# Transforming back the Hyena convolution by time parity, with frequencies f and 255-f folded on the vector engine

## The chip, the cores and the metric

One core of one Trainium2 chip. The metric is the device time of one execution in microseconds (us), the median of several runs. A core has five engines with queues of their own: TensorE (PE, with its weight loads shown apart as PEld), VectorE (DVE), ScalarE (ACT), GpSimd (POOL) and SyncE (SP), which here issues the loads of weights.

## The reference

Two layers of an encoder over 256 tokens of width 2048. Each layer runs three mixers on the same stream (an S5 state-space scan, an order-2 Hyena long convolution, latent attention), gates and lifts their outputs, and ends in a LayerNorm. The change lies in the Hyena mixer alone:

```python
def hyena_mixer(u3, conv_w, conv_b, filt_f, bias):
    uc = short_conv3(u3, conv_w, conv_b)
    v, x1, x2 = jnp.split(uc, 3, axis=-1)
    z = v
    for n, gate in enumerate((x1, x2)):
        z_f = jnp.fft.rfft(z, n=2 * L, axis=1)
        conv = jnp.fft.irfft(z_f * filt_f[:, n], n=2 * L, axis=1)[:, :L]
        z = gate * (conv + bias[n] * z)
    return z
```

Here L is 256 and there are 1024 channels. The kernel does not call an FFT: it multiplies by tables of cosines and sines at the 256 odd half frequencies (f + 0.5) / 512, which gives the same linear convolution.

## The kernel before

**Weights and the planner of the stages.** All weights come as 184 blocks per layer of 128 x 2048 numbers. SyncE loads each block as two halves into a ring of four half-slots. ScalarE rounds each quarter (128 x 512) of a block to a high part WH (`make_wh`, L370), VectorE subtracts it from the block to get the low part WL (`make_wl`, L384), and only when a half's low part stands may TensorE use that half; TensorE then makes three products for each tile (high by high, high by low, low by high; L1481). WH and WL are single buffers of four quarters. So ScalarE can write a quarter of the next block only when TensorE has used that quarter of this block (`parts_used`), and VectorE follows ScalarE. The order of the work on every engine is written out by hand; nothing is scheduled at run time.

**The Hyena stage.** Its work is spread over 24 steps `k`, each with one block of the lift (48 matmuls) behind it: 12 steps for each of the two convolutions, `o = k // 12`, `s_ = k % 12`. The stages of one convolution by step are: filter taps (0, 3), their transform (2, 5), the transposes of z (6), the forward transform of z (7 to 9), and the inverse transform (10, 11). The 256 frequencies lie as two halves `m` of 128 partitions, the 1024 channels as two halves of 512 columns. On TensorE a step is: the Hyena matmuls of the step, then the block of the step. On VectorE a step is: the low parts of quarters 0 and 1 of the next block, the Hyena work of the step, the low parts of quarters 2 and 3, and then more Hyena work (short convolutions) and every third step `mix_in`.

**What the change touches.** `product(o, m, half)` (L949 to L969) multiplies the transform of z, which lies in two PSUM banks, by the filter's transform: four products of 128 x 512 (L961 to L964), a sum (L966) and a difference (L968), into YRE and YIM. It is called four times for each convolution: for m = 0 in step 7, for m = 1 and channel half 0 in step 8, for m = 1 and half 1 in step 9. `inverse(o, n)` on TensorE (L1785 to L1798) is called in steps 10 and 11 for four of the eight tiles of channels each. It waits until all eight results of the convolution's products stand, and makes four float32 matmuls for each tile, with 128 channels as stationary operand and a table of 256 time steps as moving one (L1793). A float32 matmul shows as two records in the trace. `unconv(o, m)` on VectorE reads each finished tile from its bank in steps 10 and 11: bias (L978), scale and add (L980), gate (L984, or L987 and L988). The next user of the banks waits for L980. `put` at the end of the kernel fills the tables in the constants CON, which GpSimd's queue loads at the start (L414).

Matmuls that only release a semaphore do it through `pending`: the release rides on the next matmul that is issued. The last quarter of a block is so given back by the first matmul of what follows the block.

Of the kernel before, what the change touches and what calls it, by code (L numbers as in the profile page):

```python
# [30 lines left out]
ALU = mybir.AluOpType  # L31
# [3 lines left out]
P = 128  # L35
# [76 lines left out]
    "out":  [2, 2, 2, 2, 2, 2, 2, 2],  # L112
}
ZIN = 24 + WT
DVE_STEPS, DVE_S5_STEPS = 457, 23
ACT_STEPS, ACT_S5_STEPS = 8, 1
PER_LAYER = [sum(FILLS[s][b] for s in STAGES) for b in range(8)]

# [13 lines left out]
def columns(*parts):  # L132
    at, out = 0, {}
    for name, n in parts:
        out[name] = (at, at + n)
        at += n
    return out, at
# [3 lines left out]
                   ("conv_w0", 24), ("conv_w1", 24), ("conv_w2", 24), ("conv_b", 24), ("hy_bias", 16),  # L141
                   ("q_norm", 4), ("kv_norm", 4), ("ln_g", DT), ("ln_b", DT),
                   ("b1", 1), ("b2", 1), ("freq0", 1), ("freq1", 1))
CP, CP_N = columns(("cos", 2 * T), ("sin", 2 * T), ("icos", 2 * T), ("isin", 2 * T), ("token4", HOPS),
                   ("ident", P), ("ones", P), ("inv_freq", 1),
                   ("half_pi", 1))

# [30 lines left out]
def trunk(nc, x, blocks, lp, bc, w1, w2, b3, decay, feats, pT, pos, consts, out):  # L178
    with ExitStack() as ctx:
# [35 lines left out]
        def con(name):  # L215
            return CON[:, CP[name][0]:CP[name][1]]
# [7 lines left out]
        xh, xl = split(XH, DT), split(XL, DT)  # L224
        xx = XX[:].rearrange("p (r k t) -> p r k t", r=2, k=DT)
        dft_cos, dft_sin = con("cos").rearrange("p (k f) -> p k f", k=2), con("sin").rearrange("p (k f) -> p k f", k=2)
        idft_cos, idft_sin = con("icos").rearrange("p (k f) -> p k f", k=2), con("isin").rearrange("p (k f) -> p k f", k=2)
        ident, ones, half_pi, token4 = con("ident"), con("ones"), con("half_pi"), con("token4")


# [258 lines left out]
        def _(dve):  # L489
# [14 lines left out]
            with dve.Fori(0, DEPTH) as layer:  # L504
# [445 lines left out]
                def product(o, m, half):  # L950

                    b = 4 + 2 * half
                    n = hyc(o, "fwd", m, b)
                    n2 = hyc(o, "fwd", m, b + 1)
                    zc, zs = bank[b][:, :], bank[b + 1][:, :]
                    oc = slice(half * CW, (half + 1) * CW)
                    fr, fi = frt[:, m, oc], fit[:, m, oc]
                    t1, t3 = TM[:, 0:CW], TM[:, CW:2 * CW]
                    full(b, "hyc", n)
                    full(b + 1, "hyc", n2)  # L960
                    st.did(v.tensor_tensor(yret[:, m, oc], zc, fr, ALU.mult))  # L961
                    free(v.tensor_tensor(yimt[:, m, oc], zc, fi, ALU.mult), b)
                    st.did(v.tensor_tensor(t1, zs, fi, ALU.mult))
                    free(v.tensor_tensor(t3, zs, fr, ALU.mult), b + 1)  # L964
                    st.wait()
                    v.tensor_tensor(yret[:, m, oc], yret[:, m, oc], t1, ALU.add).then_inc(yf_ready, 1)  # L966
                    out_of(b + 1, "hyc", n2)
                    v.tensor_tensor(yimt[:, m, oc], yimt[:, m, oc], t3, ALU.subtract).then_inc(yf_ready, 1)  # L968
                    dve.wait_ge(yf_ready, layer * 16 + (o * 8 + m * 4 + half * 2 + 2))  # L969

                def unconv(o, m):

                    b, n = 4 + m % 4, hyc(o, "inv", m // 4, 4 + m % 4)
                    z, gate, t = bct[:, m, :], bct[:, 8 * (o + 1) + m, :], TM[:, 0:T]
                    if o and m:

                        dve.wait_ge(yb_ready, layer * 8 + m)
                    st.did(v.tensor_scalar(t, z, par("hy_bias", o * 8 + m), None, ALU.mult)); st.wait()  # L978
                    full(b, "hyc", n)
                    free(v.scalar_tensor_tensor(out=t, in0=bank[b][:, 0:T], scalar=NS[:, o * 8 + m:o * 8 + m + 1], in1=t,  # L980
                                                op0=ALU.mult, op1=ALU.add), b)
                    out_of(b, "hyc", n)
                    if o == 0:
                        v.tensor_tensor(z, t, gate, ALU.mult).then_inc(z_in, 1)  # L984
                        dve.wait_ge(z_in, layer * ZIN + (16 + m + 1))
                    else:
                        st.did(v.tensor_tensor(t, t, gate, ALU.mult)); st.wait()  # L987
                        v.tensor_tensor(z, t, PROJt[:, 42 + m, :], ALU.mult).then_inc(yb_ready, 1)  # L988
# [11 lines left out]
                for k in range(24):  # L1000
                    o, s_ = k // 12, k % 12
                    make_wl(dve, v, layer, B_LIFT + 24 + k + 1, halves=(0,))

                    if s_ in (0, 3):
                        taps_out(o, s_ // 3)
                    if s_ == 1 and o == 0:

                        dve.wait_ge(yh_ready, layer * 4 + 2)
                        v.tensor_tensor(YCL, YC, YCH.bitcast(F32), ALU.subtract).then_inc(yl_ready, 1)
                    if s_ in (7, 8, 9):  # L1010
                        if s_ == 8:
                            full(6, "hyc", hyc(o, "sums", 0, 6))
                            free(v.reciprocal(NS[:, o * 8:o * 8 + 8], bank[6][:, 0:8]), 6)
                        product(o, (0, 1, 1)[s_ - 7], (0, 0, 1)[s_ - 7])
                    if s_ in (10, 11):
                        for m in range((s_ - 10) * 4, (s_ - 10) * 4 + 4):
                            unconv(o, m)
                    if o == 0:
                        for m in {1: (0,), 2: (1, 2), 4: (4, 5), 5: (6, 7), 6: (9, 10)}.get(s_, ()):
                            short_conv(m)  # L1020
                    else:
                        for m in {1: (17, 18), 2: (19, 20), 4: (21, 22), 5: (23,)}.get(s_, ()):
                            short_conv(m)
                    make_wl(dve, v, layer, B_LIFT + 24 + k + 1, halves=(1,))

                    if s_ in (0, 3):
                        even_odd(o, s_ // 3)
                    if s_ in (1, 4):
                        sums(o, s_ // 3)
                    if s_ == 7:  # L1030
                        product(o, 0, 1)
                    if o == 0:
                        for m in {2: (3,), 5: (8,), 6: (11,), 8: (12,), 9: (13, 14, 15), 11: (16,)}.get(s_, ()):
                            short_conv(m)
                    if k % 3 == 2:
                        mix_in(k // 3, "hyc", k // 3)
# [384 lines left out]
        def _(pe):  # L1421
# [6 lines left out]
            with pe.Fori(0, DEPTH) as layer:  # L1428
# [355 lines left out]
                        done(ins, b)  # L1784

                def inverse(o, n):
                    pe.wait_ge(yf_ready, layer * 16 + (o * 8 + 8))
                    for c in range(4 * n, 4 * n + 4):
                        b = 4 + c % 4
                        take_bank(b, "hyc", hyc(o, "inv", n, b))  # L1790
                        for k in range(4):
                            r, m = k // 2, k % 2
                            ins = mm(bank[b][:, 0:T], yft[r][:, m, c * P:(c + 1) * P], (idft_sin if r else idft_cos)[:, m, :],  # L1793
                                     start=(k == 0), stop=(k == 3))
                            if k < 3:
                                release(ins)
                        done(ins, b)
# [173 lines left out]
def shape_constants():  # L1971

    con = np.zeros((P, CP_N), np.float32)

    def put(name, a):
        con[:, CP[name][0]:CP[name][1]] = a
    t, f = np.arange(T)[:, None], np.arange(T)[None, :]
    ang = 2 * np.pi * (f + 0.5) * t / (2 * T)
    fold = lambda a: a.reshape(2, P, T).transpose(1, 0, 2).reshape(P, 2 * T)
    put("cos", fold(np.cos(ang)))  # L1980
    put("sin", fold(np.sin(ang)))
    put("icos", fold(np.cos(ang.T) / T))
    put("isin", fold(-np.sin(ang.T) / T))
    put("token4", STEP * np.arange(HOPS))
    put("ident", np.eye(P))
    put("ones", 1.0)
    half = 32
    inv = np.float32(10000.0) ** (-np.arange(half, dtype=np.float32) / np.float32(half))
    put("inv_freq", np.tile(inv, 4)[:, None])
    put("half_pi", HALF_PI)  # L1990

    n_ch = 2 * W
    tl = np.linspace(0.0, 1.0, T, dtype=np.float32)[:, None]
    w = np.float32(2.0 * math.pi) * np.arange(T, dtype=np.float32)[:, None] / np.float32(T)
    bands = np.linspace(1e-4, 15, 16, dtype=np.float32)[None, :]
    feats = np.concatenate([tl, np.cos(bands * w), -np.sin(bands * w)], axis=-1).astype(np.float32)
    deltas = np.linspace(math.log(0.01) / 1.5, math.log(0.01) / 0.3, n_ch, dtype=np.float32)
    decay = np.exp(-tl * np.abs(deltas)).astype(np.float32)
    decay = decay.reshape(2, P, CHUNKS, CW).transpose(2, 1, 0, 3).reshape(CHUNKS, P, 2 * CW)
    return con, np.ascontiguousarray(feats.T), np.ascontiguousarray(decay)  # L2000
# [61 lines left out]
```

## Time and profile before

| | us |
|---|---|
| median of 3 runs (2844.43 to 2846.63) | 2844.88 |
| the profiled execution, its own time | 2844.58 |
| its span, first to last instruction | 2842.3 |
| TensorE busy | 2696.7 (95%) |
| VectorE busy | 1860.9 (65%) |
| ScalarE busy | 1310.6 (46%) |
| mean granted TensorE clock | 0.979 of full |

Lines of the page are read as: source line, engine, operation, output from inputs, count, busy time, mean duration of one in ns, and the idle time just before with what ended it. "WL L384" as a releaser is a low part of a weight block.

### The profile page before, as it was taken

Reading aid. Unit: us, or ns where it says so; the run is one execution under the profiler, and the core shown is the slowest. Engines: PE = TensorE matmul, PEld = TensorE weight load, DVE = VectorE, ACT = ScalarE, POOL = GpSimd, SP = SyncE. Lnnn points to the kernel's source line nnn. Section 1 sums busy time; section 2 is a strip of 40 time slices with the busy share of each in tenths; the row PEclk is TensorE's granted clock in tenths of the full one; section 3 lists DMA queues with packets and bytes.
Section 4 is the critical chain, followed back from the end, with each engine's and each line's share of the span. In section 5 each row is a group of like instructions: output and inputs, shape, how many; then the busy total and the mean of one; then the engine's idle time right before and its main releaser. Section 6 shows DMA issues by size and latency. Waiting matters only on the chain.

```text
span 2842.3 us, 49160 instructions
## 1 busy us (share of the span) xinstructions
PE 2696.7 (95%) x17320; PEld 2385.5 (84%) x17320; DVE 1860.9 (65%) x3290; ACT 1310.6 (46%) x2353; POOL 109.5 (4%) x202
## 2 busy tenths in 40 slices
PE   5899999989999999999979999999899999999998
PEld 4798999877997778998768899998789877799986
DVE  5878878734557766556577877876345677665655
ACT  3455555534554233453444555556245432334535
POOL 1100000000000000000021000000000000000000
PEclk9999999999999999999989999999999999999999
DMA  6444444423443333555554444443344523245554
GB/s 210 155 150 148 146 149 144 146 106 135 149 158 118 104 100 120 184 177 172 163 171 146 147 150 145 150 142 120 135 133 143 170 97 112 98 134 180 178 173 146
DMA packets 115388, 412.30 MB, mean 145 GB/s; under 512 B 15332, under 2 KB 15354, under 8 KB 114736
## 3 DMA queue, kind: packets, MB, share of 16 engines
q1 hardware_dynamic: 106992, 391.17, 41.2%
q0 software_dynamic: 8256, 19.26, 2.1%
q8 instruction: 89, 1.46, 0.2%
q14 instruction: 51, 0.42, 0.1%
HBM read 404.07 MB, written 6.29 MB: 144 GB/s over the span
## 4 chain that ended last, share of the span: by engine, by line
PE 87%; DVE 6%; issue 3%; ACT 3%; DMA 1%; DVEq 0%; POOLq 0%; POOL 0%; ACTq 0%; SPq 0%
PE bank L1481 30%; PE bank L1509 18%; PE bank L1511 9%; PE bank L1858 6%; PE bank L1463 5%; PE bank L1793 2%; PE bank L1602 2%; PE bank L1579 2%; PE bank L1561 2%; PE bank L1757 2%; PE bank L1780 1%; PE bank L1546 1%; PE bank L1596 1%; PE bank L1670 1%; DVE WL L384 1%
## 5 line engine op out<-in xcount | busy, mean ns | idle before, releaser
L370 ACT ACTIVATE WH<-ring 128x512 fp32r<-128x512 f32 x1364 | 858.2, 631 | 1277.1 <-PE bank L1481 599.4
L384 DVE TENSOR_TENSOR WL<-ring,WH 128x512 fp32r<-128x512 f32 x852 | 577.5, 690 | 528.9 <-ACT WH L370 526.3
L1509 PE MATMUL bank<-XX,WH 128*128 128x512 f32 x2304 | 825.5, 401 | 61.1 <-DVE XX L502 23.3
L1481 PE MATMUL bank<-XX,WH 128*128 128x256 f32 x3712 | 682.8, 286 | 13.0 <-DVE WL L384 8.5
L1511 PE MATMUL bank<-XX,WL 128*128 128x256 f32 x2304 | 646.0, 280 | 0.0
L1481 PEld LDWEIGHTS bank<-XX,WH 128*128 128x128 f32 x3712 | 580.5, 192 | 31.2 <-issue 24.3
L1509 PEld LDWEIGHTS bank<-XX,WH 128*128 128x128 f32 x2304 | 437.5, 190 | 163.8 <-issue 36.2
L1481 PE MATMUL bank<-XX,WL 128*128 128x256 f32 x1856 | 526.2, 284 | 0.0
L375 DVE TENSOR_TENSOR WL<-ring,WH 128x512 fp32r<-128x512 f32 x512 | 350.9, 688 | 139.9 <-ACT WH L370 135.9
L1511 PEld LDWEIGHTS bank<-XX,WL 128*128 128x128 f32 x2304 | 439.5, 191 | 0.0
L1481 PEld LDWEIGHTS bank<-XX,WL 128*128 128x128 f32 x1856 | 357.0, 192 | 0.0
L1463 PE MATMUL bank<-ARENA,ring 128*128 128x256 f32 x704 | 158.8, 388 | 19.4 <-ACT ARENA L1288 17.5
L1463 PEld LDWEIGHTS bank<-ARENA,ring 128*128 128x128 f32 x704 | 135.0, 195 | 42.6 <-issue 21.8
L1858 PE MATMUL bank<-WL,MIXH 128*128 128x512 f32 x256 | 101.7, 397 | 0.0
L1858 PE MATMUL bank<-WH,MIXL 128*128 128x512 f32 x256 | 101.2, 395 | 0.0
L1858 PE MATMUL bank<-WH,MIXH 128*128 128x512 f32 x256 | 101.2, 395 | 0.0
L1481 PE MATMUL bank<-YCH,WH 128*128 128x256 f32 x256 | 79.0, 309 | 0.0
L1481 PE MATMUL bank<-YAH,WH 128*128 128x256 f32 x256 | 75.0, 293 | 0.0
L1481 PE MATMUL bank<-YCL,WH 128*128 128x256 f32 x256 | 74.6, 291 | 0.0
L1481 PE MATMUL bank<-YCH,WL 128*128 128x256 f32 x256 | 74.5, 291 | 0.0
L1481 PE MATMUL bank<-YAH,WL 128*128 128x256 f32 x256 | 71.9, 281 | 0.0
L1481 PE MATMUL bank<-YAL,WH 128*128 128x256 f32 x256 | 71.9, 281 | 0.0
(299 smaller groups left out, 3561.2 us busy)
## 6 DMA issues: line engine op xcount, KB each, us to landing
ring<-in_blocks SPq DMA_DIRECT2D x738, 512.0 KB, 3.3
ARENA<-in_bc POOLq DMA_DIRECT2D x2, 2048.0 KB, 8.1
ARENA<-in_decay POOLq DMA_DIRECT2D x8, 512.0 KB, 4.6
ARENA<-in_x SPq DMA_DIRECT2D x1, 2048.0 KB, 9.4
u_scratch<-ARENA POOLq DMA_DIRECT2D x16, 128.0 KB, 2.5
ARENA<-u_scratch POOLq DMA_DIRECT2D x64, 32.0 KB, 2.9
y_scratch<-ARENA POOLq DMA_DIRECT2D x16, 128.0 KB, 2.0
ARENA<-y_scratch POOLq DMA_DIRECT2D x64, 32.0 KB, 2.7
```

Source lines behind the costliest of these rows:

```text
L370: nc.scalar.activation(wh[q], raw(which[0], q), ACT.Copy).then_inc(wh_ready[q], 1)
L375: nc.vector.tensor_tensor(wl[q], raw(which[0], q), wh[q].bitcast(F32), ALU.subtract).then_inc(w_used[slot(which[0], q // 2)], 1)
L384: vec.tensor_tensor(wl[q], raw(which[0], q), wh[q].bitcast(F32), ALU.subtract).then_inc(w_used[slot(which[0], half)], 1)
L1463: ins = mm(o, w[:, (w0 + i) * P:(w0 + i + 1) * P], rhs(i), start=i == 0, stop=i == k - 1)
L1481: ins = mm(o, w_, x_, start=start and i == 0 and n == 0, stop=stop and i == 7 and n == 2)
L1509: ins = mm(bank[b][:, :], h, xx[:, :, k, :], start=(k == 0), stop=(k == DT - 1), skip_group_check=True)
L1511: ins = mm(bank[b][:, 0:T], l, xh[:, k, :], start=False, stop=(k == DT - 1), skip_group_check=True)
L1561: ins = mm(o, ET[:, q % 2 * CW + i * P:q % 2 * CW + (i + 1) * P], u4(q), start=True, stop=True)
L1579: ins = mm(bank[4 + d][:, q * P:(q + 1) * P], b, f, start=(r == 0), stop=(r == 1))
L1602: ins = mm(o, f, x_, start=False, stop=(d == 1 and r == 1))
L1757: ins = mm(bank[4 + q][:, :], tab, ED[:, (im * 2 + t) * CW:(im * 2 + t + 1) * CW], start=(t == 0), stop=(t == 1))
L1858: ins = mm(bank[b][:, :], x_[:, k, tok[t]], w_[q], start=False, stop=(k == 15 and n == 2), skip_group_check=True)
```

## The change

The table columns of frequency are reordered, so that partition p of the first half holds frequency p and partition p of the second half holds frequency 255 - p. After the product of the second half, `fold` replaces the two halves of YRE by their sum and by the first minus the second, and the same for YIM: two additions and two scaled additions of 128 x 512 for each half of the channels. The inverse then makes even time steps from the one and odd time steps from the other: for each tile of channels four float32 matmuls as before, but with 128 moving columns each, the even steps to the first 128 columns of the bank and the odd steps to the second. `unconv` reads them in the interleaved order again. The inverse of a half of the channels now waits for that half's fold alone, and the inverse tables are half as large.

```diff
-CP, CP_N = columns(("cos", 2 * T), ("sin", 2 * T), ("icos", 2 * T), ("isin", 2 * T), ("token4", HOPS),
+CP, CP_N = columns(("cos", 2 * T), ("sin", 2 * T), ("icos", T), ("isin", T), ("token4", HOPS),
...
                     st.wait()
-                    v.tensor_tensor(yret[:, m, oc], yret[:, m, oc], t1, ALU.add).then_inc(yf_ready, 1)
+                    st.did(v.tensor_tensor(yret[:, m, oc], yret[:, m, oc], t1, ALU.add))
                     out_of(b + 1, "hyc", n2)
-                    v.tensor_tensor(yimt[:, m, oc], yimt[:, m, oc], t3, ALU.subtract).then_inc(yf_ready, 1)
-                    dve.wait_ge(yf_ready, layer * 16 + (o * 8 + m * 4 + half * 2 + 2))
+                    st.did(v.tensor_tensor(yimt[:, m, oc], yimt[:, m, oc], t3, ALU.subtract))
+                    st.wait()
+
+                def fold(o, half):
+
+                    oc = slice(half * CW, (half + 1) * CW)
+                    for y in (yret, yimt):
+                        st.did(v.tensor_tensor(y[:, 0, oc], y[:, 0, oc], y[:, 1, oc], ALU.add))
+                    for back, y in ((1, yret), (0, yimt)):
+                        st.wait(back)
+                        v.scalar_tensor_tensor(out=y[:, 1, oc], in0=y[:, 1, oc], scalar=-2.0, in1=y[:, 0, oc],
+                                               op0=ALU.mult, op1=ALU.add).then_inc(yf_ready, 1)
...
-                    free(v.scalar_tensor_tensor(out=t, in0=bank[b][:, 0:T], scalar=NS[:, o * 8 + m:o * 8 + m + 1], in1=t,
-                                                op0=ALU.mult, op1=ALU.add), b)
+                    by_parity = t.rearrange("p (s r) -> p s r", r=2)
+                    free(v.scalar_tensor_tensor(out=by_parity, in0=bank[b][:, 0:T].rearrange("p (r s) -> p s r", r=2),
+                                                scalar=NS[:, o * 8 + m:o * 8 + m + 1], in1=by_parity, op0=ALU.mult, op1=ALU.add), b)
...
                         product(o, (0, 1, 1)[s_ - 7], (0, 0, 1)[s_ - 7])
+                        if s_ > 7:
+                            fold(o, s_ - 8)
...
-                    pe.wait_ge(yf_ready, layer * 16 + (o * 8 + 8))
+                    pe.wait_ge(yf_ready, layer * 8 + (o * 4 + 2 * n + 2))
...
                         for k in range(4):
-                            r, m = k // 2, k % 2
-                            ins = mm(bank[b][:, 0:T], yft[r][:, m, c * P:(c + 1) * P], (idft_sin if r else idft_cos)[:, m, :],
-                                     start=(k == 0), stop=(k == 3))
+                            odd, r = k // 2, k % 2
+                            cols = slice(odd * P, (odd + 1) * P)
+                            ins = mm(bank[b][:, cols], yft[r][:, odd ^ r, c * P:(c + 1) * P], (idft_sin if r else idft_cos)[:, cols],
+                                     start=(r == 0), stop=(r == 1))
...
+    order = np.concatenate([np.arange(P), 255 - np.arange(P)])
+    by_parity = np.concatenate([np.arange(0, T, 2), np.arange(1, T, 2)])
+    put("cos", fold(np.cos(ang)[:, order]))
+    put("sin", fold(np.sin(ang)[:, order]))
+    put("icos", np.cos(ang.T)[:P, by_parity] / T)
+    put("isin", -np.sin(ang.T)[:P, by_parity] / T)
```

The number of counted VectorE steps in a layer (`DVE_STEPS`) goes from 457 to 481 with it.

## Rows read from the trace of the kernel before

**Rows 1.** The page: busy time of each engine, share of the span, instructions.

```profile
PE 2696.7 (95%) x17320; PEld 2385.5 (84%) x17320; DVE 1860.9 (65%) x3290; ACT 1310.6 (46%) x2353; POOL 109.5 (4%) x202
```

**Rows 2.** The page: shares by engine of the chain that ended last.

```profile
PE 87%; DVE 6%; issue 3%; ACT 3%; DMA 1%; DVEq 0%; POOLq 0%; POOL 0%; ACTq 0%; SPq 0%
```

**Rows 3.** Instruction groups by line and shape, whole span: busy us, mean ns, idle.

```profile
L384 DVE TENSOR_TENSOR WL<-ring,WH 128x512 fp32r<-128x512 f32 x852 | 577.5, 690 | 528.9 <-ACT WH L370 526.3 <-DVE ARENA L547 0.7 <-DVE ARENA L900 0.6
...
L1793 PE MATMUL bank<-CON,ARENA 128*128 128x256 f32 x256 | 58.9, 389 | 9.5 <-DVE ARENA L968 9.5
...
L769 DVE TENSOR_TENSOR_SCAN ARENA<-ARENA 128x256 f32<-128x256 f32 x64 | 40.5, 675 | 0.0
...
L729 DVE SCALAR_TENSOR_TENSOR ARENA<-ARENA 64x640 f32<-64x640 f32 x32 | 26.1, 816 | 0.5
...
L980 DVE SCALAR_TENSOR_TENSOR ARENA<-bank,NS,ARENA 128x256 f32<-128x256 f32 x32 | 15.5, 484 | 1.5
...
L968 DVE TENSOR_TENSOR ARENA<-ARENA 128x512 f32<-128x512 f32 x16 | 10.9, 684 | 0.0
```

**Rows 4.** PE timeline, layer 0, o = 1: start, length, work, [idle before, releaser].

```profile
1064.97 3.60 PE L1780 MATMUL bank<-ARENA,CON 128*128 128x512 f32 x8
...
1076.67 7.17 PE L1793 MATMUL bank<-CON,ARENA 128*128 128x256 f32 x32 [2.36 <-DVE ARENA L968]
...
1089.43 7.20 PE L1793 MATMUL bank<-CON,ARENA 128*128 128x256 f32 x32
...
1108.80 0.58 PE L1481 MATMUL bank<-XX,WH 128*128 128x256 f32 x2 [2.77 <-DVE WL L384]
```

**Rows 5.** Windows: length, then PE, PEld, DVE, ACT, POOL busy, clock, DMA.

```profile
933.81:976.21 42.40, 39.69 (x239) 33.56 (x239) 31.95 (x66) 9.34 (x16) 0.00 (x0) 1.00 0.26 88
1063.83:1108.06 44.23, 39.20 (x251) 34.73 (x250) 30.02 (x62) 9.37 (x16) 0.00 (x0) 1.00 0.26 84
2340.64:2383.02 42.38, 39.69 (x239) 33.57 (x239) 31.95 (x65) 9.35 (x16) 0.00 (x0) 1.00 0.27 88
2470.66:2516.60 45.94, 40.83 (x251) 35.85 (x249) 30.08 (x62) 9.35 (x16) 0.00 (x0) 0.96 0.24 81
```

**Rows 6.** DVE timeline, layer 0, o = 0: its waits in that stretch.

```profile
948.04 0.69 DVE L384 TENSOR_TENSOR WL<-ring,WH 128x512 fp32r<-128x512 f32 x1 [0.80 <-ACT WH L370]
...
955.94 0.69 DVE L384 TENSOR_TENSOR WL<-ring,WH 128x512 fp32r<-128x512 f32 x1 [2.87 <-ACT WH L370]
957.50 0.69 DVE L384 TENSOR_TENSOR WL<-ring,WH 128x512 fp32r<-128x512 f32 x1 [0.87 <-ACT WH L370]
...
968.60 0.69 DVE L384 TENSOR_TENSOR WL<-ring,WH 128x512 fp32r<-128x512 f32 x1 [3.64 <-ACT WH L370]
970.14 0.69 DVE L384 TENSOR_TENSOR WL<-ring,WH 128x512 fp32r<-128x512 f32 x1 [0.85 <-ACT WH L370]
```

**Rows 7.** Timeline of DVE: two of the products in a row.

```profile
1064.39 0.68 DVE L962 TENSOR_TENSOR ARENA<-bank,ARENA 128x512 f32<-128x512 f32 x1
1064.98 0.68 DVE L963 TENSOR_TENSOR ARENA<-bank,ARENA 128x512 f32<-128x512 f32 x1
```

**Rows 8.** Timeline of PE in the S5 stage: float32 matmuls of 128 columns.

```profile
126.43 1.95 PE L1579 MATMUL bank<-ARENA 128*128 128x128 f32 x16
128.13 0.48 PE L1509 MATMUL bank<-XX,WH 128*128 128x512 f32 x1
```

**Rows 9.** Timeline of PE, layer 1, o = 1: the first inverse.

```profile
2483.46 8.86 PE L1793 MATMUL bank<-CON,ARENA 128*128 128x256 f32 x32 [2.36 <-DVE ARENA L968]
```

**Rows 10.** Windows: granted clock (PEclk) behind two waits of PE.

```profile
1107.00:1112.00 5.00, 3.20 (x16) 3.20 (x17) 4.86 (x10) 3.35 (x4) 0.55 (x1) 0.71 0.37 125
2483.00:2489.00 6.00, 5.54 (x18) 4.60 (x19) 1.71 (x3) 0.90 (x2) 0.00 (x0) 0.72 0.25 87
```

**Rows 11.** DMA issues at the start: KB, us from issue to landing.

```profile
ARENA<-in_x SPq DMA_DIRECT2D x1, 2048.0 KB, 9.4
...
CON<-in_consts POOLq DMA_DIRECT2D x1, 1185.0 KB, 10.8
```

More of the change, by code:

```diff
@@ L114 @@
 ZIN = 24 + WT
-DVE_STEPS, DVE_S5_STEPS = 457, 23
+DVE_STEPS, DVE_S5_STEPS = 481, 23
 ACT_STEPS, ACT_S5_STEPS = 8, 1
@@ L226, in trunk @@
         dft_cos, dft_sin = con("cos").rearrange("p (k f) -> p k f", k=2), con("sin").rearrange("p (k f) -> p k f", k=2)
-        idft_cos, idft_sin = con("icos").rearrange("p (k f) -> p k f", k=2), con("isin").rearrange("p (k f) -> p k f", k=2)
+        idft_cos, idft_sin = con("icos"), con("isin")
         ident, ones, half_pi, token4 = con("ident"), con("ones"), con("half_pi"), con("token4")
@@ L1979, in shape_constants @@
     fold = lambda a: a.reshape(2, P, T).transpose(1, 0, 2).reshape(P, 2 * T)
[L1980 to L1983, printed above, removed]
+    order = np.concatenate([np.arange(P), 255 - np.arange(P)])
[4 more added lines that the diff above has]
+    put("isin", -np.sin(ang.T)[:P, by_parity] / T)
     put("token4", STEP * np.arange(HOPS))
```

## Prediction

> **What bounds the kernel now.** I read the page first: TensorE is busy 95% of the span, VectorE 65% [rows 1], and the chain that ended last is 87% TensorE and 6% VectorE [rows 2]. So over the whole span a us taken from TensorE is worth nearly a us. That is an average, and the change sits in four short places: two layers, two convolutions each, steps 8 to 12. There the reader is to look at two things. In the timeline of TensorE, the first inverse of a convolution waits 2.36 us for the last subtraction of `product` (L968), and soon after the second inverse TensorE waits 2.77 us for a low weight part, WL, from VectorE [rows 4]. And in the windows from the product of step 8 to the end of the last `unconv`, VectorE is busy 31.95 of 42.4 us in the first convolution (o = 0) and 30.0 of 44.2 or 45.9 us in the second (o = 1), well above its share of 65% [rows 5]. So these stretches have two lines of work of nearly one length. TensorE takes 39.7 us in the one and VectorE 32.0 us plus the waits for WH that TensorE's pace gives it [rows 5, 6]. A cut on TensorE alone is given back only until VectorE's idle time in the stretch is used up.
>
> **TensorE: half the columns.** The inverse is 128 instructions in 256 records, 58.9 us busy [rows 3], in eight calls of 32 records; an undisturbed one shows 7.17 us with a tail of 0.4 [rows 4], so 6.8 us. The count stays, with 128 columns instead of 256. The S5 stage has float32 matmuls of just that shape, 128 x 128 by 128 columns, each with its own weights: 16 records start at 126.43 and the next work starts at 128.13, 0.106 us a record [rows 8]. So a call takes 32 x 0.106 = 3.4 us and saves 3.4 us. That the weight loads don't become the bound is shown by the same row, which has one load for each record too.
>
> **TensorE: the wait before the first inverse.** It needed the products of step 9; now it needs only the fold of step 8, which ends about 2.4 us later than the product of step 8 does now, more than 3 us before TensorE is through with the block of step 9. The 2.36 us go. The wait also held back the release of the block's last quarter, which rides on the first matmul of the inverse. The second inverse needs the fold of step 9, which ends while TensorE is in the block of step 10. If nothing else were late, one convolution would gain 2.36 + 2 x 3.4 = 9.2 us.
>
> **VectorE: the folds.** Each fold is two additions and two scaled additions of 128 x 512. A step from one product to the next is 0.60 us [rows 7], and a scaled addition costs what an addition does: 640 columns in 816 ns against 512 in 684 to 690 is 1 ns a column [rows 3]. The waits in it are for the instruction before the last, or one whose result is due when its turn comes, at 0.1 us or less. The drain behind the last subtraction was there before. So 2.4 us a fold, 4.8 us a convolution, 19.2 us in all. The stretch from the product of step 8 onward takes both folds.
>
> **What the two together give.** With both folds in, I follow VectorE through one stretch (o = 0, layer 0), each instruction at its present length. Fold 0 moves everything behind it by 2.4 us, so the last low part of the block of step 9 stands at about 941.2, just before TensorE needs it. Fold 1 puts the low parts of quarters 2 and 3 for the block of step 10 about a us behind TensorE's need. From there every wait for WH of VectorE is gone: it comes to each after ScalarE has been there. The four waits of `unconv`'s time vanish, and TensorE instead waits for VectorE, about 1 us in the block of step 10 and 2.7 us in that of step 11. So the stretch gets shorter by VectorE's waits less the folds. The waits of o = 0 are five: 0.80 + 2.87 + 0.87 + 3.64 + 0.85 = 9.03 us [rows 6]. The window has 42.40 - 31.95 = 10.45 us idle [rows 5]; the other 1.4 us are the small gaps between dependent instructions, which stay. The same difference in the other windows gives 14.21 - 1.4 = 12.8 (layer 0, o = 1), 10.43 - 1.4 = 9.0 (layer 1, o = 0) and 15.86 - 1.4 = 14.5 (layer 1, o = 1). Less 4.8 each: 4.2 + 8.0 + 4.2 + 9.7 = 26.1 us. This is below TensorE's 9.2 in each (in the last TensorE also gets back a slow piece of clock, below), so VectorE is the bound. Behind the stretches both engines stand as far from each other as now: the taps of o = 1 follow the last `unconv` of o = 0 as before, and the 2.77 us wait after o = 1 stays, or grows to about 3.3 us.
>
> **The read by parity.** L980 reads its bank with a hop of 128 numbers after each and takes 484 ns now, 32 times [rows 3]. No row has such a read. Below, nothing is lost: the count of elements is the same (a gain is excluded, since no element is saved). Above, the nearest rows are those of an instruction that takes two cycles or so an element: the scan, 675 ns for 256 columns [rows 3], against the 425 ns that 684 ns for 512 come to with 1 ns a column: 0.25 us more. The read's own row stands at the lower end, the only slow row at the upper, and neither is nearer in kind, so I take the middle, 0.125 us. VectorE is the bound there, so all count: 32 x 0.125 = 4.0 us, bounds 0 and 8.0.
>
> The Trainium skill (Vector Engine (DVE) Microarchitecture Reference, section 5.2, "The SBUF access granule: adjacent pairs") speaks against the edit: a port streams at full rate only while its elements come in adjacent pairs, and one source that hops every element cost 1.73 instead of 1.054 ns a column. It says so of SBUF; here the source is PSUM, which no row shows. By it each read would cost 0.17 us more (an estimate from that page), 5.5 us in all instead of 4.0, and the time would be 2825.6.
>
> **The clock.** After the wait of 2.36 us in layer 1, o = 1 the inverse shows 8.86 us instead of 7.17 [rows 9], and the granted clock is 0.72 over that window: part of it at the lower level, 1.2 GHz. The wait of 2.77 us is followed by the same (0.71) [rows 10]. The first is already in the 9.7 above. New waits of up to 2.7 us in the block of step 11 of o = 0, in both layers, may bring one each: 2 x 1.7 us. As VectorE is the bound there, I count half: 1.7 us lost, bounds 0 and 3.4.
>
> **The constants.** CON shrinks by 512 of 2370 columns, 256 of 1185 KB. The whole load took 10.8 us [rows 11] in a time when the queues share the bandwidth; at 0.4 MB/us for all of them, as 2 MB of x, the first weights and this arrive in some 12 us, 0.25 MB are 0.6 us at most. The first work waits for it; I take 0.4 us, bounds 0 and 0.6.
>
> The semaphores and the host's reordering of tables cost nothing. The forward transform has the same instructions with other table columns.
>
> **The sum.** 26.1 + 0.4 - 4.0 - 1.7 = 20.8 us less. The profiled execution took 2844.58 us, with 2842.3 us of span, 0.3 us under the median of 2844.88; I count from the median: 2824.1 us. Its own range, from the bounds of the terms: 2844.9 - 26.7 = 2818 to 2844.9 - (26.1 - 8.0 - 3.4) = 2830.
>
> **The rivals.**
> - *TensorE keeps its whole cut.* If VectorE's work can move off the path (the folds hide in its waits and the low parts still come in time), 4 x 9.2 + 1.7 + 0.4 = 38.9 us, 2806. For it: TensorE is 95% busy. Against it: the waits of VectorE (9.0) are less than 4.8 + 9.2. 6%.
> - *Half width doesn't halve the time.* If a record of the inverse is held by something like the weight load's own length, 0.19 us instead of 0.106, a call takes 6.1 us and a convolution gains 2.36 + 2 x 0.7 = 3.8 us: 15.2 + 1.7 + 0.4 = 17.3, less about 2 of the parity read that the slack doesn't hide, 2830. Against it: [rows 8]. The edit then does not do what it says. 7%.
> - *The clock.* Each of the waits that now fall on TensorE (two to each convolution) starts a piece at the lower level, at 1.7 us, all on the path: six more than counted, 10 us, so 2834. For it: both rows of [rows 10]. Against it: the waits of 2.36 us of [rows 4] cost nothing. 16%.
> - *Slower: the loop of WH and WL.* ScalarE's high part waits for TensorE, VectorE's low part for ScalarE, TensorE for VectorE. If the added work on VectorE delays each turn of that loop and the waits for WH stay as they are, they are not idle time to be used, and folds and parity reads are added whole: 19.2 + 4.0 = 23 us, 2868. It decides when less than 5.8 us of a stretch's 9.0 to 14.5 us of waits can be used. For it: VectorE's waits all name ScalarE [rows 6]. Against it: ScalarE is busy only 9.3 us in each stretch [rows 5], and its own wait is for TensorE, which comes sooner. 5%.
>
> **How the numbers follow.** The forecast has 66%. Range 2814 to 2834: the forecast with its bounds, the clock's case to its value, and part of the first rival's way; outside are the loop, most of the first rival and the far half of the clock. A run of this kernel can tell 0.2%, 5.7 us, from no change. Below 2839 lie the forecast, the first two rivals and nearly all of the clock's case: faster 91%. Within 0.2%: 5%, the far end of the clock's case and a mild form of the loop. Slower: 4%.
>
> **What would show it.** L1793 at 256 records and about 31 us busy instead of 58.9 (half width right; 48 would be the second rival). No wait before the first inverse. VectorE idle in the four windows down to the small gaps of 1.4 us, with the waits on L370 gone and waits of TensorE on "WL L384" in their place in the blocks of steps 10 and 11: the bound has changed hands. The fold's four instructions at 0.69 us each, 32 in all of 22 us busy. L980 at 0.6 us if the middle is right, 0.48 or 0.73 at the ends. If VectorE still has several us of waits in the windows and TensorE has none, the first rival is right; if both have waits, the loop is.

## The result and the profile after

The changed kernel takes 2827.94 us (median of 4 runs, 2823.75 to 2829.64) against 2845.29 us before (4 runs): ratio 0.9936, 95% interval 0.9919 to 0.9954. That is 17.4 us or 0.6% faster. Two later groups of five runs gave 2827.27 and 2824.77 us, ratios 0.9940 (0.9926 to 0.9953) and 0.9925 (0.9911 to 0.9938). The profiled execution is the shortest of the first four: 2823.75 us, 20.8 us less than the profiled execution before. Its span is 2822.2 us, 20.1 us less. So its trace shows some 3 us more of gain than the medians.

The page, busy time of each engine (compare [rows 1]), and the chain that ended last (compare [rows 2]):

```profile
PE 2676.2 (95%) x17320; PEld 2370.0 (84%) x17320; DVE 1878.4 (67%) x3322; ACT 1310.4 (46%) x2353; POOL 109.5 (4%) x202
...
PE 85%; DVE 8%; issue 3%; ACT 3%; DMA 1%; DVEq 0%; POOLq 0%; POOL 0%; ACTq 0%; SPq 0%
```

TensorE lost 20.5 us of busy time, VectorE gained 17.5, and the chain moved by 2% from the one to the other. The groups of instructions that changed (compare [rows 3]; the inverse is now L1807, the read by parity L991, the folds L975 and L978):

```profile
L1807 PE MATMUL bank<-CON,ARENA 128*128 128x128 f32 x256 | 37.1, 304 | 12.4 <-DVE ARENA L991 11.3 <-DVE ARENA L962 1.0
...
L991 DVE SCALAR_TENSOR_TENSOR ARENA<-bank,NS,ARENA 128x256 f32<-128x256 f32 x32 | 15.5, 483 | 1.5
...
L975 DVE TENSOR_TENSOR ARENA<-ARENA 128x512 f32<-128x512 f32 x16 | 10.3, 688 | 0.3
L978 DVE SCALAR_TENSOR_TENSOR ARENA<-ARENA 128x512 f32<-128x512 f32 x16 | 10.3, 685 | 0.0
```

The first line has the surprise: the 9.5 us of waits for L968 before the inverse are gone, and 12.4 us of waits are there instead, 11.3 of them for L991, which is `unconv`, and 1.0 for L962, which is `product`. The timeline of TensorE places them (first convolution of layer 0, then the second; compare [rows 4]):

```profile
943.15 1.95 PE L1807 MATMUL bank<-CON,ARENA 128*128 128x128 f32 x16
945.60 2.35 PE L1807 MATMUL bank<-CON,ARENA 128*128 128x128 f32 x16 [0.50 <-DVE ARENA L962]
...
958.05 6.70 PE L1807 MATMUL bank<-CON,ARENA 128*128 128x128 f32 x32 [3.80 <-DVE ARENA L991]
```

```profile
1072.35 3.73 PE L1807 MATMUL bank<-CON,ARENA 128*128 128x128 f32 x32
...
1083.43 1.16 PE L1807 MATMUL bank<-CON,ARENA 128*128 128x128 f32 x8 [0.41 <-DVE ARENA L991]
1085.34 1.16 PE L1807 MATMUL bank<-CON,ARENA 128*128 128x128 f32 x8 [0.76 <-DVE ARENA L991]
1087.17 1.16 PE L1807 MATMUL bank<-CON,ARENA 128*128 128x128 f32 x8 [0.67 <-DVE ARENA L991]
...
1100.50 0.70 PE L1494 MATMUL bank<-XX,WH 128*128 128x256 f32 x2 [2.81 <-DVE WL L384]
```

An undisturbed call is 3.73 us, 0.24 of it tail, where it was 7.17: the columns were halved and so was the time. But both calls of a convolution write banks 4 to 7. The first call of the first convolution stops for 0.50 us in its middle, for a bank that the product of step 9 (L962) has not read out yet. And the second call may write a bank only when `unconv` has read the first call's tile from it. In the first convolution `unconv` stands on VectorE behind three short convolutions (4.4 us), and TensorE waits 3.80 us for it. The call behind this wait takes 6.70 us instead of 3.73, because of the clock. Windows of the two such places, layer 0 and layer 1 (length, then PE, PEld, DVE, ACT and POOL busy, granted clock, DMA share, GB/s; compare [rows 10]):

```profile
958.00:962.00 4.00, 3.95 (x18) 3.95 (x19) 3.60 (x9) 0.90 (x2) 0.00 (x0) 0.50 0.36 131
2357.00:2361.00 4.00, 3.91 (x22) 3.91 (x23) 3.60 (x10) 0.90 (x2) 0.00 (x0) 0.61 0.39 131
```

0.50 is the lower of the clock's two levels, 1.2 GHz, for the whole window. Finally the four stretches from the product of step 8 to the end of the last `unconv` (compare [rows 5]):

```profile
932.85:974.49 41.64, 36.63 (x240) 31.56 (x240) 36.49 (x74) 9.35 (x16) 0.00 (x0) 0.92 0.25 89
1062.08:1099.78 37.70, 33.12 (x251) 30.03 (x249) 34.39 (x70) 9.34 (x16) 0.00 (x0) 1.00 0.30 98
2331.87:2372.20 40.33, 35.32 (x240) 30.24 (x239) 36.49 (x74) 9.34 (x16) 0.00 (x0) 0.96 0.28 92
2458.29:2496.01 37.72, 33.17 (x251) 30.08 (x250) 34.41 (x70) 9.35 (x16) 0.00 (x0) 1.00 0.31 98
```

They are 157.4 us together, 174.95 before: 17.6 us less, of the 20.1 us by which the span shrank. The gain is very uneven: 0.8 and 2.1 us in the first convolutions, 6.5 and 8.2 us in the second. VectorE is busy 4.3 to 4.5 us more in each. Its idle time is 5.15, 3.31, 3.84 and 3.31 us; with 1.3 to 1.4 of small gaps in each, 3.7, 2.0, 2.4 and 2.0 us are still waits. The forecast had none left. They stand behind the bank wait, and they are waits for WH, as before. The longest in the first stretch:

```profile
966.86 0.69 DVE L384 TENSOR_TENSOR WL<-ring,WH 128x512 fp32r<-128x512 f32 x1 [2.90 <-ACT WH L370]
```

### The profile page after: what moved, and what is told of

It is laid out like the page before. It is cut to its first block, busy times and chain, and to the rows that moved or that the text cites. A ratio compares the mean times of both kernels' runs of the same rounds, so it can differ in the third digit from the quotient of the medians.

```text
span 2822.2 us, 49206 instructions
## 1 busy us (share of the span) xinstructions
PE 2676.2 (95%) x17320; PEld 2370.0 (84%) x17320; DVE 1878.4 (67%) x3322; ACT 1310.4 (46%) x2353; POOL 109.5 (4%) x202
## 4 chain that ended last, share of the span: by engine, by line
PE 85%; DVE 8%; issue 3%; ACT 3%; DMA 1%; DVEq 0%; POOLq 0%; POOL 0%; ACTq 0%; SPq 0%
PE bank L1494 29%; PE bank L1522 18%; PE bank L1524 9%; PE bank L1872 6%; PE bank L1476 5%; PE bank L1615 2%; PE bank L1592 2%; PE bank L1574 2%; PE bank L1770 2%; DVE WL L384 1%; PE bank L1793 1%; PE bank L1559 1%; PE bank L1609 1%; PE bank L1683 1%; PE bank L1708 1%
## 5 line engine op out<-in xcount | busy, mean ns | idle before, releaser
L1476 PE MATMUL bank<-ARENA,ring 128*128 128x256 f32 x704 | 158.8, 387 | 18.7 <-ACT ARENA L1301 17.4
```

What stands on the lines that cost most here:

```text
L1476: ins = mm(o, w[:, (w0 + i) * P:(w0 + i + 1) * P], rhs(i), start=i == 0, stop=i == k - 1)
```

## The experiments

Three groups, each on one chip with runs of the kernel before beside them. "Under before" is the difference of the medians of a group.

| run | median us | under before | ratio, 95% interval |
|---|---|---|---|
| a1_after_again | 2827.27 | 17.4 | 0.9940, 0.9926 to 0.9953 |
| a2_split_wait | 2834.08 | 10.6 | 0.9962, 0.9949 to 0.9976 |
| a3_no_fold | 2814.40 | 30.3 | 0.9895, 0.9879 to 0.9910 |
| a4_wide | 2840.93 | 3.7 | 0.9985, 0.9976 to 0.9994 |
| b1_after_third | 2824.77 | 20.7 | 0.9925, 0.9911 to 0.9938 |
| b2_late | 2827.00 | 18.5 | 0.9931, 0.9918 to 0.9945 |
| b3_banks | 2816.52 | 29.0 | 0.9896, 0.9881 to 0.9912 |
| b4_banks_late | 2818.67 | 26.8 | 0.9904, 0.9888 to 0.9919 |
| c1_banks_again | 2814.41 | 31.6 | 0.9890, 0.9874 to 0.9905 |
| c2_banks_no_fold | 2807.43 | 38.5 | 0.9868, 0.9853 to 0.9883 |
| c3_banks_pool | 2823.44 | 22.5 | 0.9921, 0.9907 to 0.9934 |
| c4_sbuf_hop | 2824.05 | 21.9 | 0.9923, 0.9908 to 0.9938 |

**The changed kernel again.**

> The changed kernel once more, as the reference point of this group. Its runs so far spread from 2823.8 to 2829.6 us. Both theories: 17 to 21 us under the kernel before. If the spread is that of pieces at the lower TensorE clock, the profile with more such pieces is the longer one, 1.7 us for each 3.4 us piece.

17.4 us under before. The spread came again, 2823.6 to 2832.5 us. That it is the clock's was not shown: this profile has a span 2.3 us longer than the first one and no more time at the lower level (mean granted clock 0.978 in both). 3.0 us of the difference lie between the Hyena stretches of layer 0 and those of layer 1, where the kernel was not changed; the cause stays open.

**The split wait alone**, in the kernel before.

```diff
-                    pe.wait_ge(yf_ready, layer * 16 + (o * 8 + 8))
+                    pe.wait_ge(yf_ready, layer * 16 + (o * 8 + 6 + 2 * n))
```

> The kernel before with one line changed: the inverse of a half of the channels waits for that half's products alone; no folds, full-width inverse. Theory (VectorE bounds the stretches behind the products, and the banks of the inverse are given back by unconv): the 2.36 us wait before each first inverse goes, VectorE has 9 to 14.5 us of waits to follow with, so about 2.3 us each, 9 us in all, and the slow clock piece of layer 1 with it or moved: 7 to 11 us faster than the kernel before. Rival (the gain of the whole change is mainly this wait): 15 us or more.

10.6 us, within what the theory gave. The line of the inverse in its trace:

```profile
L1793 PE MATMUL bank<-CON,ARENA 128*128 128x256 f32 x256 | 56.8, 380 | 0.0
```

No wait is left before it, where [rows 3] has 9.5 us. So one changed number gives 10.6 us, and everything else in the change together adds 6.8. The stretches show where: here they are 39.9, 41.7, 39.8 and 41.6 us. In the second convolutions the rest of the change takes off another 4 us each. In the first it makes them longer, 41.6 and 40.3 us: there the folds and the bank wait cost more than the halved columns give.

**Without the folds.** `fold` is not called, and `product` releases YRE and YIM as before; this kernel leaves out part of the transform.

```diff
-                        if s_ > 7:
-                            fold(o, s_ - 8)
```

> The changed kernel without its folds: half-width inverse, split wait, read by parity, but the 8 folds of 4 instructions are left out (their part of the computation is missing). Theory (VectorE bounds): the 19.2 us of the folds come back nearly whole, up to TensorE's own 9.2 us a convolution: 15 to 19 us faster than the changed kernel, 35 to 39 us faster than the kernel before. Rival (TensorE bounds, the folds are hidden and the shortfall lies in clock pieces): within 3 us of the changed kernel.

12.9 us faster than the changed kernel: far from the rival's 3, but under the 15 to 19 expected. The four stretches are 145.8 us together, 11.6 less than with the folds. TensorE's waits before the inverse, from the list of waits (who waited for whom, us in total, times, longest):

```profile
PE bank L1805 <- DVE ARENA L991: 6.3, 14, 0.8
```

14 waits of at most 0.8 us: without folds the second inverse still follows `unconv` tile by tile. That this is what holds it was tested further down: with two tiles in a bank and no folds the stretches are 137.6 us, 8.3 less again, and these waits are gone.

**Full width.** Only the halving of the columns is undone; what the inverse gives is then not the transform.

```diff
-                            ins = mm(bank[b][:, cols], yft[r][:, odd ^ r, c * P:(c + 1) * P], (idft_sin if r else idft_cos)[:, cols],
+                            ins = mm(bank[b][:, 0:T], yft[r][:, odd ^ r, c * P:(c + 1) * P], (idft_sin if r else idft_cos)[:, 0:T],
```

> The changed kernel with full-width inverse matmuls (256 columns each, whole table), so only the halving of the columns is undone; what the inverse gives is not the transform. TensorE does 27 us more work in the eight calls. Theory (VectorE bounds, and TensorE waits 3.8 us in each first convolution and 1.8 us in each second for banks, and 2.8 us behind the second): about half is hidden in these waits: 10 to 17 us slower than the changed kernel. Rival (TensorE bounds): 25 to 28 us slower.

13.7 us slower than the changed kernel. TensorE has 27 us more to do; half of it costs nothing. The four stretches grow by 13.4 us (its profiled run is the slowest of its eleven, 5.8 us above their median, so only the stretches are compared). The same list shows what most of the half that costs nothing replaced:

```profile
PE bank L1806 <- DVE ARENA L991: 4.2, 2, 2.1
```

11.3 us of waits in eight became 4.2 in two, and the 1.0 us for L962 is gone. So the halved columns are real on TensorE, and of the half of them that is given back 8.1 us are waits for banks. The rest was not separated; the slow clock behind the long waits is part of it.

**The changed kernel, third group.**

> The changed kernel, as the reference point of this group: 17 us under the kernel before, as in the first group. Its profile is to show the two waits of about 3.8 us of the second inverse for L991, each followed by a piece at the lower clock.

20.7 us under before. Both waits of 3.8 us are in its trace, with a low piece of 3.4 us behind each (the first profile had 6.8 in layer 0), and its stretch there is 40.3 us instead of 41.6.

**The short convolutions later.**

```diff
-                        for m in {2: (3,), 5: (8,), 6: (11,), 8: (12,), 9: (13, 14, 15), 11: (16,)}.get(s_, ()):
+                        for m in {2: (3,), 5: (8,), 6: (11,), 8: (12,), 10: (13, 14, 15), 11: (16,)}.get(s_, ()):
```

> The changed kernel with the short convolutions 13, 14 and 15 (4.4 us of VectorE) moved from step 9 to behind the first four unconv of step 10, so that unconv gives the banks back 4.4 us sooner in the first convolution of each layer. Theory (the second inverse waits for banks that unconv holds, and this wait then brings the slow clock): both waits of 3.8 us and the slow pieces behind them go; VectorE's remaining waits in these stretches are 3.7 and 2.4 us, so 3 to 6 us faster than the changed kernel. Rival (VectorE's amount of work alone is the bound, whatever its order): within 1.5 us.

A miss: 2.2 us slower than the changed kernel, which is no more than the spread of either's runs (4 us), and surely not 3 to 6 faster. The waits of 3.8 us went, and the first stretches shortened to 37.7 us, with VectorE idle only in its small gaps. But the short convolutions now stand before the last four `unconv`, and the taps of the next convolution take the same banks. Timeline and window of this kernel:

```profile
966.23 1.12 PE L1755 MATMUL bank<-ARENA 64*128 64x512 f32 x2 [1.27 <-DVE ARENA L994]
...
968.97 2.08 PE L1755 MATMUL bank<-ARENA 64*128 64x512 f32 x4 [0.41 <-DVE ARENA L994]
```

```profile
965.00:982.00 17.00, 15.35 (x46) 9.10 (x46) 10.14 (x23) 1.55 (x3) 0.56 (x1) 0.60 0.28 93
```

The wait moved to the taps (L1755, for L994, which is `unconv` there), and behind it the granted clock is 0.60 over 17 us. In layer 1 the taps wait as long, 1.32 us, and the clock is 0.90 over the same 17 us. From the end of the first stretch to the start of the second the kernel now needs 92.0 and 89.2 us in the two layers, where the changed kernel of this group needs 86.1. What the stretch won, 2.6 us in each, was lost after it.

**Two tiles in a bank.** The first inverse fills banks 4 and 5, the second 6 and 7; `unconv` frees a bank after its second tile. Its core:

```diff
-                        b = 4 + c % 4
-                        take_bank(b, "hyc", hyc(o, "inv", n, b))
+                        b = 4 + c // 2
+                        if c % 2 == 0:
+                            take_bank(b, "hyc", hyc(o, "inv", n, b))
...
-                            ins = mm(bank[b][:, cols], yft
+                            ins = mm(bank[b][:, c % 2 * T + odd * P:c % 2 * T + (odd + 1) * P], yft
```

> The changed kernel with two tiles of the inverse in each bank: the first inverse fills banks 4 and 5, the second 6 and 7, so that no inverse waits for unconv. VectorE's order is unchanged. Theory (banks): the waits of the second inverse go, 3.8 us in each first convolution and 1.8 us in each second; VectorE's waits in the stretches (3.7, 2.0, 2.4, 2.0 us) bound the gain: 5 to 10 us faster than the changed kernel. Rival (VectorE's work alone): within 1.5 us, the wait moving to the low parts WL.

8.3 us faster than the changed kernel, 2816.5 us: the fastest so far of the kernels that compute everything. Its inverse, and what TensorE waits for around it (layer 0, first convolution):

```profile
944.26 3.73 PE L1812 MATMUL bank<-CON,ARENA 128*128 128x128 f32 x32
...
952.24 0.50 PE L1498 MATMUL bank<-XX,WH 128*128 128x256 f32 x2 [1.38 <-DVE WL L384]
...
955.20 3.73 PE L1812 MATMUL bank<-CON,ARENA 128*128 128x128 f32 x32
...
964.55 0.36 PE L1498 MATMUL bank<-YCH,WH 128*128 128x256 f32 x1 [2.76 <-DVE WL L384]
```

Both calls run undisturbed (the 0.50 us for L962 are gone too), and TensorE waits 1.38 and 2.76 us for low parts in the blocks of steps 10 and 11: the waits that the prediction named there, about 1 and 2.7 us. The windows of its first two stretches:

```profile
933.97:971.81 37.84, 33.70 (x239) 29.89 (x239) 36.40 (x74) 9.34 (x16) 0.00 (x0) 0.95 0.30 98
1057.57:1093.16 35.59, 32.58 (x251) 29.88 (x249) 34.32 (x70) 9.28 (x16) 0.00 (x0) 1.00 0.32 104
```

VectorE is idle 1.44 and 1.27 us, its small gaps and nothing else. It is a bound here; whether it is the only one, the run without folds below tells.

**Both edits.**

> Both edits. Theory: they remove the same wait in the first convolutions, so together little more than the better of the two, up to 2 us, from the low parts of the block of step 11 that come sooner: 6 to 11 us faster than the changed kernel. Rival (VectorE's work alone): within 2 us of the changed kernel.

6.1 us faster than the changed kernel, 2.2 slower than the two-bank version. The stretches are as short (37.7 and 35.7 us), and again the taps wait, 1.98 us, with a low clock behind. Order alone does not shorten what VectorE already fills.

**The two-bank version again.**

> The two-tiles-a-bank version once more, as the reference point of this group: 28 to 30 us faster than the kernel before, VectorE without a wait for WH in the four stretches, 37.8 us long in the first convolutions and 35.6 us in the second.

31.6 us under before, a little more than the 28 to 30 expected, with stretches of 37.8 and 35.7 us.

**Two banks, no folds.**

> Two tiles a bank, and the folds left out (their part of the computation is missing). Theory (with the banks out of the way VectorE's work is the bound): the folds' 4.8 us a convolution come back until TensorE bounds, at 9.2 us a convolution under the kernel before: 33.2 and 35 us stretches, 9 to 13 us faster than the two-bank version. Rival (something else bounds that version): under 4 us.

7.0 us faster than the two-bank version, less than the 9 to 13 expected and above the rival's 4. The first convolutions are 33.3 us, 4.5 less, and VectorE has hardly a wait in them; the second are 35.5 us, 0.2 less than with the folds, and VectorE has 4.2 us of waits again. So in the second convolutions TensorE's line of work is as long as VectorE's: the folds of the two-bank version cost something only in the first.

**GpSimd makes half of the folds.** The sum of the imaginary halves goes to free columns of FIM.

```diff
+                        g.tensor_tensor(IMS[:, oc], y[:, 0, oc], y[:, 1, oc], ALU.add).then_inc(yp_ready, 1)
+                        g.tensor_tensor(y[:, 1, oc], y[:, 0, oc], y[:, 1, oc], ALU.subtract).then_inc(yp_ready, 1)
```

> Two tiles a bank, and GpSimd makes the imaginary half of each fold (an addition into free columns of FIM and a subtraction), VectorE the real half: the same computation. No row shows GpSimd adding, so its time is open. Theory (VectorE's work is the bound): 1.2 us less on VectorE for each of 8 folds, 5 to 9 us faster than the two-bank version if GpSimd needs under 3 us for its two and VectorE keeps its pace. Rival (the two engines slow each other, or the inverse waits for GpSimd): no gain, or up to 10 us slower.

9.0 us slower than the two-bank version, the rival's side. Groups of its trace:

```profile
L458 POOL TENSOR_TENSOR ARENA<-ARENA 128x512 f32<-128x512 f32 x8 | 13.8, 1725 | 0.0
L457 POOL TENSOR_TENSOR ARENA<-ARENA 128x512 f32<-128x512 f32 x8 | 13.3, 1658 | 304.5 <-DVE ARENA L979 304.5
```

```profile
L993 DVE SCALAR_TENSOR_TENSOR ARENA<-ARENA 128x512 f32<-128x512 f32 x8 | 13.3, 1657 | 0.3
```

GpSimd's addition takes 1.66 us. VectorE's own scaled addition, which runs beside it, takes 1657 ns where the same instruction takes 685 without GpSimd. The two low parts behind it take 2.38 us instead of 1.29. So VectorE lost more by the slowing than it saved by two instructions a fold: it is busy 38.1 us in the first stretches, 1.7 more than with both folds of its own, and fills them. TensorE has no wait for GpSimd in this trace, so the other half of the rival, an inverse that waits for GpSimd, did not occur. The four stretches are 153.9 us, 7.0 more than in the two-bank version.

**The hop in SBUF.**

```diff
-                    st.did(v.tensor_scalar(t, z, par("hy_bias", o * 8 + m), None, ALU.mult)); st.wait()
+                    st.did(v.tensor_scalar(t.rearrange("p (s r) -> p s r", r=2), z.rearrange("p (r s) -> p s r", r=2),
+                                           par("hy_bias", o * 8 + m), None, ALU.mult)); st.wait()
```

> The changed kernel with the interleave moved from the read of PSUM (L991) to the read of z from SBUF in the bias step (L988): the same hop of 128 numbers after each, the other memory; the channel's time steps come out permuted. If a hop in SBUF costs what the page on the access granule says, L988 goes from 352 to about 530 ns (an estimate from that page) and the kernel is about 4 to 6 us slower than the changed kernel; if the read of PSUM and of SBUF are alike, L988 stays at 352 ns, as the read of PSUM did at 483, and the time is the changed kernel's.

```profile
L988 DVE TENSOR_SCALAR ARENA<-ARENA,PAR 128x256 f32<-128x256 f32 x32 | 11.4, 355 | 0.9
```

355 ns against 352, and 21.9 us under before, where the changed kernel was 17.4 and 20.7 under in the other groups: the hop cost nothing in SBUF either, in an instruction with one tensor as its source. The time steps come out permuted in this kernel, so it serves for the duration alone.

## Why the prediction was right, and where it was not

The median came out 3.8 us above the 2824.1 of the forecast, in its range and on its side. The profiled execution shows just the 20.8 us of the forecast, but that is luck: it is the shortest of its four runs, and the terms below don't agree so well. Step by step:

- *Half the columns, half the time*: right. 3.73 us a call with its tail against 7.17, so 3.4 us saved, as forecast from the S5 rows. The rival of half width that doesn't halve the time (a record held at 0.19 us) is out. The sign that was named for it, L1807 at about 31 us busy, did not come: it is 37.1, since two of the eight calls run in part at the lower clock (6.70 and 5.35 us) and four are broken up by waits.
- *The wait before the first inverse goes*: right, and it was the larger part: 10.6 us when done alone. A wait for a bank, 0.5 us for L962, came inside the first call of the first convolutions in its place.
- *The folds cost 2.4 us each*: right in the instructions (688 and 685 ns, 32 of them). What they cost the kernel was measured by leaving them out: 12.9 of the 19.2 us.
- *"The second inverse needs the fold of step 9, which ends while TensorE is in the block of step 10"*: this is the step that failed. It looked at the data and not at the banks. The second inverse also needs the banks that `unconv` of the first gives back, and with TensorE's half of the race shortened and VectorE's lengthened, that became the later of the two: 11.3 us of waits, and a low clock behind the two long ones. It makes up the difference in the stretches: forecast 174.9 - 26.1 = 148.8 us (before the terms for parity read and clock), measured 157.4. The gain by stretch was forecast as 4.2, 8.0, 4.2 and 9.7 us and came out as 0.8, 6.5, 2.1 and 8.2: 5.5 of the missing 8.6 us are in the first convolutions, where the wait is 3.8 us. With the wait taken away (two tiles a bank) the stretches are 37.8 + 35.6 + 37.8 + 35.6 = 146.9 us. So the forecast's sum, waits of VectorE less the folds, was the sum of a kernel without this bank conflict, to 2 us. In the second convolutions that agreement is in part luck, since TensorE's line is as long there: without folds they shorten by 0.2 us only.
- *VectorE becomes the bound*: half right. The exchange was there (full width costs half of its 27 us), but VectorE kept 10 us of waits, since the bank wait held TensorE, and through it ScalarE's high parts. The waits of TensorE for WL of 1 and 2.7 us in the blocks of steps 10 and 11 did not come either: the changed kernel has 0.31 us in the one and none in the other, and only the two-bank version shows them.
- *The read by parity, 4.0 us*: wrong, 0. L991 takes 483 ns, [rows 3] has 484. The page that was weighed there (the Trainium skill, Vector Engine (DVE) Microarchitecture Reference, section 5.2) gave 0.17 us a read for a source that hops every element; here it is not seen, in PSUM or, with one tensor source, in SBUF. The same section says that a one-source instruction which alternated between two regions (and wrote one word for two that it read) ran at the full rate. L988 at 355 ns agrees with that, though it writes one word for each that it reads.
- *The clock, 1.7 us for pieces after new waits in the first convolutions*: the kind was right, the place was the bank wait. The first stretches of layer 0 in two profiles differ by 1.3 us (41.6 and 40.3), with 6.8 and 3.4 us of low clock. The rival in which every new wait of TensorE starts such a piece did not come true: in the second convolutions the granted clock is 1.00, with three waits of 0.4 to 0.8 us in each.
- *The constants, 0.4 us*: the first matmul started at 22.67 us, 0.6 us sooner. Of the profiles the two with the large table have it at 23.30 and 23.31 us, the twelve with the small one at 22.51 to 22.76.
- *TensorE keeps its whole cut* (38.9 us less) is out: the folds are not hidden, they cost 12.9 us.

The error of the bank wait (8.6 us too much gain) and that of the parity read (4.0 too little) have opposite signs, which is why the total looks better than its parts; that they nearly cancel is luck. Of the 20.1 us by which the span shrank, 17.6 are the stretches and 0.6 the start. Of the other 1.9, 1.5 lie between the two stretches of layer 1: the granted clock is 0.98 there before and 1.00 after, one piece at the lower level less, which other profiles of the same kernel have or lack in layer 0. It can't be put down to the change.

The case of the loop of WH and WL, in which folds and parity reads are added whole and the kernel gets slower, is out: it is faster, and VectorE's waits in the stretches fell from between 9.0 and 14.5 us to between 2.0 and 3.7. But the sign that the prediction named for it came true, waits of both engines in the stretches. The sign was badly chosen: any third resource that holds TensorE, here a bank, gives it too.

## What to carry to other kernels

When a wait for data is relaxed, list the other things that its instruction waits for, above all the buffer that it writes: the later of the two is the new wait. A pair of engines that run at nearly one length gives back part of what is taken from one of them. The sum "idle time of the partner less the work added to it" gave the stretches to 2 us here once no buffer tied the two. Try the smallest edit alone, and look at it place by place: here one number in a wait gave 10.6 of the 17.4 us, the rest of the change made two of the four stretches longer, and the packing of two tiles in a bank gave another 8.3 without one instruction less on TensorE.

## What the hardware showed that was not expected

- A VectorE read that alternates after each element between two runs 128 numbers apart cost nothing: 483 ns from PSUM (484 without), and 355 ns from SBUF (352 without) in an instruction with one tensor source.
- A GpSimd addition of 128 x 512 takes 1.66 us in the trace (spans on GpSimd are rough), and a VectorE instruction of two SBUF sources beside it stretched from 685 to 1657 ns.
- Waits of TensorE of 3.8 us were followed by 3.4 to 6.8 us at 1.2 GHz in all three profiles of the changed kernel. In the kernel with the late short convolutions 1.27 us before the taps was followed by a granted clock of 0.60 over 17 us in layer 0, and 1.32 us at the same place of layer 1 by 0.90. Of the four waits of 2.36 us before, that of [rows 9] had a piece at the lower level behind it, and the other three had none (granted clock 1.00 over their stretches, [rows 5]). So the length of the wait alone did not decide it.
